# Two products instead of three for the score maps of differential attention, their splits two slots later, and the position bias in two DMAs

## What is computed

```python
def diff_attention(q, k, v, lam):          # q, k: (..., head, 2, 64)
    sc = einsum("bqhcd,bkhcd->bchqk", q, k) * (64 ** -0.5)
    p = softmax(sc)
    a = p[:, 0] - lam * p[:, 1]            # two maps a head
    return einsum("bhqk,bkhd->bqhd", a, v)
...
bias = rpb[:, dr_i][:, :, :, dc_i]         # kind A: rpb is (8, 15, 31)
sc = where(col_ok, sc + bias, NEG_INF)
```

## Time and profile before

| | us |
|---|---|
| median of 3 runs | 1178.91 |
| the profiled execution itself | 1178.83 |
| its span, first to last instruction | 1176.6 |
| TensorE busy | 1163.8 (99% of the span) |
| VectorE busy | 736.4 (63%) |
| ScalarE busy | 583.8 (50%) |
| GpSimd busy | 121.0 (10%) |

### The profile page before, as it was taken

How to read it: one execution, slowest core, us unless ns; L and a number is a source line. 1 busy time by engine, 2 the same in 40 slices (tenths; PEclk the granted TensorE clock), 3 DMA queues, 4 the chain that set the end, 5 groups by cost and what they waited for, 6 DMA issues and landing times.

```text
span 1176.6 us, 14665 instructions
## 1 busy us (share of the span) xinstructions
PE 1163.8 (99%) x5476; PEld 972.6 (83%) x5476; DVE 736.4 (63%) x842; ACT 583.8 (50%) x745; POOL 121.0 (10%) x177
## 2 busy tenths in 40 slices
PE   8999999999999999999999999999999999999997
PEld 6888888888888888888888888888888888888886
DVE  6676566656764975764666555565746667668654
ACT  6554445544555654564545454445444444446442
POOL 2400002000000310010100101102011002002100
PEclk9999999999999999999999999999999999999999
DMA  9987666744646785455767666666765766455741
GB/s 355 242 238 251 215 227 211 232 170 152 249 148 248 176 267 184 153 205 179 248 209 228 220 201 230 207 222 197 253 201 170 249 188 228 143 182 179 258 152 72
DMA packets 86441, 245.23 MB, mean 208 GB/s; under 512 B 33729, under 2 KB 51521, under 8 KB 60913
## 3 DMA queue, kind: packets, MB, share of 16 engines
q1 hardware_dynamic: 82704, 235.44, 60.2%
q0 software_dynamic: 3392, 8.96, 2.9%
q10 hardware_dynamic: 288, 0.08, 0.0%
HBM read 221.37 MB, written 8.39 MB: 195 GB/s over the span
## 4 chain that ended last, share of the span: by engine, by line
PE 96%; DVE 2%; ACT 1%; DMA 1%; issue 0%; SPq 0%; DVEq 0%; ACTq 0%
PE acc L497 89%; PE bank_x L660 2%; PE bank_y L613 1%; DMA raw<-weights 1%; PE bank_x L656 1%; PE bank_y L602 1%; PE bank_x L644 1%; DVE w_lo L1054 1%; PE bank_y L629 0%; PE bank_x L629 0%; PE bank_y L609 0%; DVE mix L1310 0%; ACT w_hi L760 0%; DVE resid L1365 0%; DVE probs L1301 0%
## 5 line engine op out<-in xcount | busy, mean ns | idle before, releaser
L497 PE MATMUL acc<-w_hi,act_hi 128*128 128x512 f32 x1560 | 615.8, 395 | 3.8 <-DVE w_lo L1054 3.8
L497 PE MATMUL acc<-w_lo,act_hi 128*128 128x512 f32 x1560 | 608.7, 390 | 0.0
L1054 DVE TENSOR_TENSOR w_lo<-raw,w_hi 128x2048 fp32r<-128x2048 f32 x195 | 449.0, 2305 | 180.6 <-ACT w_hi L760 180.4
L760 ACT ACTIVATE w_hi<-raw 128x2048 fp32r<-128x2048 f32 x195 | 373.5, 1916 | 298.7 <-PE acc L497 282.3
L497 PE MATMUL acc<-w_hi,act_lo 128*128 128x512 f32 x1560 | 418.2, 390 | 0.0
L497 PEld LDWEIGHTS acc<-w_hi,act_hi 128*128 128x128 f32 x1560 | 293.4, 188 | 62.1 <-issue 3.5
L497 PEld LDWEIGHTS acc<-w_hi,act_lo 128*128 128x128 f32 x1560 | 293.3, 188 | 62.2 <-DVE act_lo L1072 0.4
L497 PEld LDWEIGHTS acc<-w_lo,act_hi 128*128 128x128 f32 x1560 | 293.5, 188 | 57.3
L767 ACT ACTIVATE unit<-acc,pre_r 128x512 f32<-128x512 f32 x78 | 49.4, 685 | 123.0 <-PE acc L497 119.8
L440 POOL TENSOR_TENSOR rope_c<-unit,cst 128x256 f32<-128x256 f32 (+1 forms) x19 | 14.1, 740 | 728.0 <-ACT unit L767 596.2
L1213 DVE TENSOR_SCALAR mix<-bank_x 128x256 f32<-128x256 f32 (+1 forms) x24 | 10.1, 421 | 65.8 <-PE bank_x L660 65.8
(11 more groups left out here) (179 smaller groups left out, 619.6 us busy)
## 6 DMA issues: line engine op xcount, KB each, us to landing
raw<-weights SPq DMA_DIRECT2D x195, 1024.0 KB, 5.0
qk_raw<-postg SPq DMA_DIRECT2D x176, 64.0 KB, 2.1
p_moved<-p_blocks SPq DMA_DIRECT2D x16, 256.0 KB, 5.5
probs<-p_moved SPq DMA_DIRECT2D x64, 64.0 KB, 1.9
mix<-rpb POOLq DMA_DIRECT2D x32, 64.0 KB, 22.4
postg<-post_g POOLq DMA_DIRECT2D x2, 1024.0 KB, 8.0
resid<-x_perm POOLq DMA_DIRECT2D x2, 1024.0 KB, 8.6
p_moved<-p_blocks SPq DMA_DIRECT2D x16, 128.0 KB, 5.0
```

The lines of the kernel that those rows point to most:

```text
L497: m = nc.tensor.matmul(tiles[t][:, :], a[:, kt, t * P:(t + 1) * P], w[:, buf, kk * NB:(kk + 1) * NB], start=(kt == 0 and a is act_hi and w ...
L760: nc.scalar.activation(w_hi[:, at % SPLIT, :], raw[:, at % RAW, :], ACT.Copy).then_inc(S["hi_ready"], 1)
L1054: nc.vector.tensor_tensor(w_lo[:, at % SPLIT, :], raw[:, at % RAW, :], w_hi[:, at % SPLIT, :].bitcast(F32), ALU.subtract).then_inc(S["lo_r ...
```

## The change

Kind B's maps come from two matmuls a query tile. The stationary operand of map `c` is `q_hi[:, c]`, with the high part of q on the map's own 64 partitions and its low part on the other 64. The moving operand of the first matmul, over 128 partitions, is `both_k[:, c, 0]`, the high part of k on both halves. The second matmul reads the map's own 64 partitions alone: the high part of q by the low part of k. ScalarE makes the high parts in slot 3, after `split_hi` of step 1, in six copies of 64 partitions; VectorE makes the low parts in slot 4, after `split_lo` of step 1, in four subtractions of 64 partitions. Map `c` waits for its own pair. The zeros and their semaphore are gone. The bias comes in two DMAs, each 64 partitions x 8 heads of one run of 219 numbers, from which VectorE reads the overlapping windows.

```diff
@@ -50,6 +50,7 @@
 GRID_W = 64
 ROWS = SEQ // GRID_W
 RPB_R, RPB_C = 15, 31
+BIAS_RUN = (ROWS - 1 + 2 * (NT - 1)) * RPB_C + GRID_W
 SCALE = HEAD ** -0.5
 SCALE_B = (HEAD // 2) ** -0.5
 LAMBDA_INIT = 0.2
@@ -152,7 +153,7 @@
         act_lo = sb("act_lo", [P, KT, SEQ], F32R)
         unit = sb("unit", [P, 3, NT, NB])
         mix = sb("mix", [P, NT, D_MODEL])
-        with nc.sbuf_tensor("split_q", [P, 2, 2, NT * UH, P], F32R) as split_q:
+        with nc.sbuf_tensor("both_k", [P, 2, 2, QUADS, NT * UH * QUAD], F32R) as both_k:
             pass
         resid = sb("resid", [P, NT, D_MODEL])
 
@@ -248,16 +249,15 @@
                  "map0_full map1_full map0_max map1_max map0_neg map1_neg map0_exp map1_exp b_inv b_w b_scaled "
                  "probs_turned p_out p_in pt_ready o_full o_squared o_taken unit_done "
                  "m_new m_diff m_exp m_wsum m_scaled "
-                 "pre_sq pre_sum pre_var pre_std pre_rdy lam_p lam_s lam_e bias_rdy "
+                 "pre_sq pre_sum pre_var pre_std pre_rdy lam_p lam_s lam_e bias_in bias_rdy "
                  "y_sq y_scaled y_sum y_var y_std y_rdy "
-                 "rs_v rs_s rs_rdy tanh_done gate_u gate_done q_zeroed").split()
+                 "rs_v rs_s rs_rdy tanh_done gate_u gate_done").split()
         S = {n: sem(n) for n in names}
         x_first = [sem(f"x_first{kt}") for kt in range(CK)]
         w_first = [sem(f"w_first{kt}") for kt in range(CK - 1)]
         x_in = {h: sem(f"x_in{h}") for h in range(2, 2 * CHUNKS)}
         x_new = [sem(f"x_new{t}") for t in range(NT)]
         landed = [sem(f"landed{i}") for i in range(RAW)]
-        bias_in_two = [sem(f"bias_in_two{i}") for i in range(UH)]
 
         def const(name):
             a, n = CONST_COLS[name]
@@ -305,6 +305,10 @@
 
             src = raw_by_tile[:, c % 2, k, :, :, :].rearrange("p t a (h b n) -> p n b (t a h)", h=2, b=4)
             return src, dst[:, c * CK + k, :].rearrange("p (n b r) -> p n b r", n=4, b=4)
+
+        def hi_count(u):
+
+            return 2 * split_units(u) + (0 if u.kind == "A" else 2 * (u.index - 2) if u.kind == "B" else 4)
 
         def split_units(u):
 
@@ -412,15 +416,12 @@
             pool.dma_start(sinkb[:, :], sink.partition_broadcast(P)).then_inc(S["vecs_in"], 16)
 
 
-            for h in range(8):
-                for t in range(NT):
-                    for half in range(2):
-                        r = 2 * t + half
-                        src = bass.AP(rpb.tensor, h * RPB_R * RPB_C + (7 - r) * RPB_C + 15 - (GRID_W - 1),
-                                      [[1, GRID_W], [RPB_C, ROWS], [1, GRID_W]])
-                        at = (h * NT + t) * SEQ
-                        pool.dma_start(bias_in[half * 64:half * 64 + 64, at:at + SEQ].rearrange(
-                            "p (j k) -> p j k", j=ROWS), src).then_inc(bias_in_two[h // 2], 16)
+            for half in range(2):
+
+                src = bass.AP(rpb.tensor, (7 - 2 - half) * RPB_C + 15 - (GRID_W - 1),
+                              [[1, GRID_W], [RPB_R * RPB_C, 8], [1, BIAS_RUN]])
+                pool.dma_start(bias_in[half * 64:half * 64 + 64, 0:8 * BIAS_RUN].rearrange("p (h n) -> p h n", h=8),
+                               src).then_inc(S["bias_in"], 16)
 
             def rotate(u, k, blk, cols, group):
 
@@ -458,11 +459,6 @@
 
                         pool.wait_ge(S["roped"], CREDIT + 2 * (u.index - 2) + k)
                         rotate(u, k, blk, cols, HEAD // 2 if layer == 0 else HEAD)
-                    if layer == 0 and u.index == 2:
-
-                        pool.wait_ge(S["masked"], 2 * UH)
-                        pool.memset(split_q[:, :, :, :, :].rearrange("p c b a n -> p (c b a n)").bitcast(F32), 0.0).then_inc(
-                            S["q_zeroed"], 1)
                 if layer == 0:
 
                     pool.wait_ge(S["qk_in"], QK_DMAS * UNITS[0])
@@ -616,8 +612,8 @@
                 m.then_inc(S["s_full"], 1)
 
             def score_map(u, j, c):
+                pe.wait_ge(S["qk_ready"], 2 * split_units(u) + c + 1)
                 if c == 0:
-                    pe.wait_ge(S["qk_ready"], 2 * split_units(u) + 2)
                     if j > 0:
 
                         pe.wait_ge(S["map0_exp"], u.diff(j))
@@ -625,10 +621,10 @@
                     if j > 0:
                         pe.wait_ge(S["o_taken"], u.head(j))
                 for t in range(NT):
-                    for n, (a, b) in enumerate(PARTS):
+                    for part, rows in enumerate((slice(0, P), slice(64 * c, 64 * c + 64))):
                         m = nc.tensor.matmul((Y, X)[c][:, t * SEQ:(t + 1) * SEQ].rearrange("p (t a c) -> p t a c", t=NT, a=QUADS),
-                                             split_q[:, c, a, t * UH + j, :],
-                                             keys_of((k_hi[:, :, :], k_lo)[b], j), start=(n == 0), stop=(n == len(PARTS) - 1))
+                                             q_hi[rows, c, t * UH + j, :], keys_of(both_k[rows, c, part, :, :], j),
+                                             start=(part == 0), stop=(part == 1))
                 m.then_inc(S[f"map{c}_full"], 1)
 
             def turn_probs(u, j):
@@ -803,11 +799,12 @@
                 act.wait_ge(S["qk_in"], QK_DMAS * u.index + QK_DMAS)
                 if u.kind == "B":
 
-                    act.wait_ge(S["q_zeroed"], 1)
                     for c in range(2):
-                        rows = slice(64 * c, 64 * c + 64)
-                        m = nc.scalar.activation(by_quads(split_q[rows, c, 0, :, :]), raw_quads(0, rows), ACT.Copy)
-                    m.then_inc(S["qk_hi"], 1)
+                        mine, other = (slice(64 * r, 64 * r + 64) for r in (c, 1 - c))
+                        nc.scalar.activation(by_quads(q_hi[mine, c, :, :]), raw_quads(0, mine), ACT.Copy).then_inc(S["qk_hi"], 1)
+                        nc.scalar.activation(both_k[other, c, 0, :, :], qk_raw[mine, :, 1, :], ACT.Copy)
+                        nc.scalar.activation(both_k[mine, c, 0, :, :], qk_raw[mine, :, 1, :], ACT.Copy).then_inc(S["qk_hi"], 1)
+                    return
                 elif u.kind == "G":
                     nc.scalar.activation(by_quads(g_q[:, :, :]), raw_quads(0), ACT.Copy).then_inc(S["g_ready"], 1)
                     return
@@ -834,7 +831,7 @@
                 if u.by_blocks:
                     for j in u.stages(h, 6):
                         order_pT(u, j)
-                if h == 2:
+                if h == (3 if u.kind == "B" else 2):
                     split_qk_hi(u)
                 if h == 4 and u.kind == "D":
 
@@ -1097,17 +1094,22 @@
                                             unit[:, blk, :, :].rearrange("p t (h j c) -> p j (t h) c", j=QUADS, c=QUAD))
                 m.then_inc(S["qk_turned"], 1)
 
+            def split_both_lo(u, c):
+
+                mine, other = (slice(64 * r, 64 * r + 64) for r in (c, 1 - c))
+                dve.wait_ge(S["qk_hi"], hi_count(u) + 2 * c + 1)
+                nc.vector.tensor_tensor(by_quads(q_hi[other, c, :, :]), raw_quads(0, mine),
+                                        by_quads(q_hi[mine, c, :, :].bitcast(F32)), ALU.subtract)
+                dve.wait_ge(S["qk_hi"], hi_count(u) + 2 * c + 2)
+                nc.vector.tensor_tensor(both_k[mine, c, 1, :, :], qk_raw[mine, :, 1, :],
+                                        both_k[mine, c, 0, :, :].bitcast(F32), ALU.subtract).then_inc(S["qk_ready"], 1)
+
             def split_qk_lo(u):
 
                 for blk in range(2):
 
-                    dve.wait_ge(S["qk_hi"], 2 * split_units(u) + blk + 1)
-                    if u.kind == "B" and blk == 0:
-                        for c in range(2):
-                            rows = slice(64 * c, 64 * c + 64)
-                            m = nc.vector.tensor_tensor(by_quads(split_q[rows, c, 1, :, :]), raw_quads(0, rows),
-                                                        by_quads(split_q[rows, c, 0, :, :].bitcast(F32)), ALU.subtract)
-                    elif blk == 0 or u.kind == "D":
+                    dve.wait_ge(S["qk_hi"], hi_count(u) + blk + 1)
+                    if blk == 0 or u.kind == "D":
                         m = nc.vector.tensor_tensor(by_quads(q_lo[:, blk, :, :]), raw_quads(blk),
                                                     by_quads(q_hi[:, blk, :, :].bitcast(F32)), ALU.subtract)
                     else:
@@ -1261,7 +1263,10 @@
             def attention(u, h):
                 if u is None:
                     return
-                if h == 3 and u.kind != "G":
+                if u.kind == "B" and h == 4:
+                    split_both_lo(u, 0)
+                    split_both_lo(u, 1)
+                if h == 3 and u.kind not in ("B", "G"):
                     split_qk_lo(u)
                 if h == 4 and u.kind == "D":
 
@@ -1443,13 +1448,16 @@
                         if layer == 0 and u is None and s >= BODY - UH:
 
                             pair = s - (BODY - UH)
```

(11 more changed lines are left out.)

## The result

The changed kernel takes 1187.87 us, the median of 4 runs (1187.22 to 1189.05), against 1179.02 us before, over 4 runs taken with them. The ratio is 1.0077, with a 95% interval of 1.0064 to 1.0089: it is slower by 8.9 us. The forecast was 1175.1 us and a range up to 1186.0. Of the profiled execution's 1187.22 us the span is 1185.4, 8.8 more than before.

What follows compares the result with a forecast made beforehand. TensorE, busy 99% of the span, was taken as the bound. 1178.83 us less 3.84 for 32 matmuls, other terms at nothing, gave 1175.0, or 1175.1 after adding 0.08 to reach the median; range 1173.2 to 1186.0.

Steps and rivals of the forecast that it cites:

- The step that failed: TensorE, maps: a 64-partition matmul costs the full-height 120 ns, with no cost at a change of height.
- The first rival: TensorE, maps: array empties at each of 64 height changes, 162 ns each, 10.4 us, ending at 1185.5; chance 0.27.
- its tail: TensorE, maps: weight load also comes after the emptying, 350 ns a change, 22.4 us, ending at 1197.5.
- Its sign: TensorE chain, if the array empties: a map takes 1.1 us, projections behind stay at 2.72 us.
- Break-even: TensorE, maps: height changes decide the outcome from 3.84 / 64 = 60 ns a change upwards.
- 32 matmuls at 0.12 us: TensorE, kind B maps of two units: 32 matmuls go at 0.12 us each, 3.84 us less.
- The splits: ScalarE and VectorE: copies take 3.1 us more a unit, subtractions 1.2 us more; pairs in time, no TensorE wait.
- the 1.5 and 2.1 us claimed: Second unit: margins by which the operand pairs of map 0 and map 1 are ready before TensorE asks.
- One sign: ScalarE: `w_hi` of step 1 starts at 228.6 in the first unit and at 303.5 in the second.
- The bias DMAs and the zeroing: DMA queues and GpSimd: both buy nothing; even issued in 19.6 us and landing 22.4 later, the bias loses nothing.
- The second rival: TensorE, maps: emptying partly hidden, 23 to 97 ns a change, balance -2.4 to +2.4 us, 1178.9; chance 0.18.
- The third: ScalarE and VectorE splits run late, TensorE waits once a unit; at worst 8.4 us, 1183.5; chance 0.05.

Runs made afterwards that it cites:

- run 1: Changed kernel with its second product over all 128 partitions, the unused half of the moving operand zeroed once by GpSimd: 1175.35 us, ratio 0.9972 to the kernel before.
- run 2: Changed kernel with a map's four matmuls reordered, both full ones then both short ones, two height changes a map: 1181.35 us, ratio 1.0019.
- run 3: Kernel before with all six matmuls of a map reading only the map's own 64 partitions: 1184.77 us, ratio 1.0052.
- run 4: Kernel before with only the last of a map's six matmuls reading 64 partitions: 1185.51 us, ratio 1.0061.
- run 9: Kernel before with one projection matmul in each of 32 slots of layer 0 reading only 64 partitions: 1191.32 us, ratio 1.0101.
- run 10: Kernel before with two projection matmuls in a row, in each of 32 layer 0 slots, both reading partitions 0 to 63: 1192.21 us, ratio 1.0111.
- run 11: Kernel before with two projection matmuls in a row in 32 layer 0 slots, one reading partitions 0 to 63, the next 64 to 127: 1184.92 us, ratio 1.0049.
- run 8: Changed kernel with a full-height second product, its other half filled by a low part of k instead of zeros, one more subtraction a map: 1177.54 us, ratio 0.9991.
- run 5: Kernel before with the bias in two DMAs and nothing else of the change: 1178.55 us, ratio 0.9994.
- run 6: Changed kernel with zero-filled full-height second products and the bias in its 32 DMAs as before: 1175.35 us, ratio 0.9968.

## Why the prediction was wrong

**The step that failed** is the price of a short matmul among full ones. The prediction took "the full-height price, 120 ns, because the nearest row speaks for it", the transposes. Those rows do show that another use of the array costs nothing, but they are of full height, `128*128` in the trace like every other matmul of the kernel before, and so they say nothing of a change of height. Taken as the nearest row they were no evidence for the size of this term. With no row for it, the range should have reached over the rival's whole price. What the runs show in its place is 0.19 us for each of the 64 changes, 12.5 us in all (runs 1 to 4 and 9), and nothing for being short as such.

**The first rival is what happened**, in its place (four changes a map, 64 in all) and in the main in its mechanism. Its price, 282 - 120 = 162 ns, was 0.03 us short: 0.196 by run 1, 0.192 by run 9. It took the 282 from a row whose end is modelled, and put the weight load either at nothing or, in its tail, at 188 ns behind the emptying. The starts divide the price otherwise. With 256 columns in front the load of the other height starts 0.21 us after the matmul in front (237.06 - 236.85), 0.09 beyond the usual distance of 0.12. With 512 columns in front it is 0.32 (97.07 - 96.75 in run 10; load and matmul rows start together there too), 0.09 beyond 0.227. The matmul follows its load by 0.10, a time that costs nothing where the load is made ahead. That gives 0.19: about half of it the load held back, half the load that stands in TensorE's way. This is a reading of start times; no run varied the load, so the division isn't shown by experiment.

With 0.195 the rival's sum would have been 1178.83 - 3.84 + 12.5 = 1187.5 us; it read 1185.5, and the range ended at 1186.0 because it took the rival at its lower price and left out all that lay above. Its sign, projections unchanged behind a map of 1.1 us, was right for the map (1.06) and wrong for the projections (2.92 for 2.77), which hold a part of the last change.

The rule of the Trainium skill that stood beside it ("TensorEngine Tiling (Array Packing)", section Key Properties) agrees with these runs in both halves: changing the mode drains TensorE, 0.19 us a time here, and changing only the tile doesn't (run 11).

**Break-even** was put at 60 ns a change for 64 changes, which is 3.84 / 32 = 120 ns for the 32 of run 2. At 0.195 run 2 should be 6.2 - 3.84 = 2.4 us slower than before, and it is by 2.7 (1181.35 - 1178.66), which agrees.

**32 matmuls at 0.12 us** was right. Run 1 gives 3.3 us by the medians of its own comparison (1178.66 - 1175.35; the interval is 2.1 to 4.6 us), and the chain charges 0.48 for a map as worked out.

**The splits** were right in place, order and outcome. First unit: six copies ended at 237.2 for 236.8 forecast, the last subtraction at 238.5 for 238.0. Of this 0.27 us is the later start of the whole stretch, the rest a distance of 1.08 us between copies instead of 1.05. The copies to the other half cost no more. No wait came of it: TensorE waits for no other engine between 200 and 380 us in the changed kernel. Run 8 shows the margins thinner than the 1.5 and 2.1 us claimed: with 1.2 and 2.4 us more of VectorE ahead of the two pairs their loads wait 0.3 and 0.5 us, where 0.3 us to spare and 0.3 us late would have followed. One sign was a slip: it names 303.5 for `w_hi` in the second unit, while the layout above it has 305.4, 8.2 us ahead of map 0. It started 8.1 ahead (310.03 for 318.10).

**The bias DMAs and the zeroing** were rightly costed at nothing. For the DMAs runs 5 and 6 show it. The zeroing wasn't tried by itself; run 1 has one of its own and still reaches the forecast's 1175.1 within 0.3 us. The DMAs were issued faster than the bound assumed:

```profile
24.33 1.40 POOL L423 DMA_DIRECT2D mix<-rpb  x2
```

1.40 us for the two, against 19.62 us for 32, and they landed 18.2 us after issue in the median.

**The second rival**, an emptying partly hidden, is excluded by the price: 0.19 us a change against its 0.023 to 0.097. **The third**, splits too late, didn't occur.

## What to carry to other kernels

Count the changes between 128 and 64 partitions in TensorE's order of work, not the short matmuls: each costs 0.19 us here, and a short matmul among its like costs what a full one does. Only changes between 128 and 64 were run, no smaller heights. Where TensorE is the bound, fill a half-height product up with zeros to full height if the zeros can be set once off the path (3.3 us faster than before instead of 8.9 slower). A wait that grows on an engine behind TensorE has to be followed through the whole row of steps up to where TensorE takes the result, not to the first one.

## What had not been expected of the hardware

Two matmuls of 64 partitions, on the two halves and into different banks, start 0.01 us apart, so that 32 such pairs cost 7.3 us less than 32 pairs on one half (run 11's expectation had left open whether they would). The price of a change doesn't depend on the columns of its neighbours: 0.19 us between maps of 256 and projections of 512, and the same among projections alone. And the profile names no releaser for it: it appears as 0.24 us of "issue" ahead of a weight load, as a load that starts together with its matmul instead of ahead of it, and as matmul rows that are about 0.11 us longer.
